# A two-layer MLP block in seven-product form on one core: the row norm ahead of it, the loads of its second phase and its last 512 hidden units rearranged

## The reference, cut to what matters

```python
x = x + y @ w_out[l]                                  # 1024 x 1024 by 1024 x 1024
xn2 = _rmsnorm(x, norm2_g[l])                          # row norm, the MLP's input
x = x + jnp.square(jax.nn.relu(xn2 @ w_up[l])) @ w_down[l]   # 1024 -> 4096 -> 1024
return _rmsnorm(x, final_g)
```

## Time and profile before

| what | value |
|---|---|
| median of 3 executions | 2787.88 us (2782.99 to 2789.32) |
| the profiled execution's own time | 2788.39 us |
| its span in the profile | 2786.6 us |
| mean granted clock of PE | 0.973 |
| output phase, second half, ends | at 2096.1 us |
| up phase, PE's last matmul | at 2429.3 us |
| down phase, first matmul | at 2437.55 us |
| PE's last matmul | at 2757.2 us |

### The profile page before, as it was taken

One profiled execution on the slowest core, in us unless ns is written; L12 is line 12 of the kernel. 1 busy time (PEld: TensorE's weight loads), 2 busy tenths in 40 slices (PEclk: granted clock), 3 DMA queues, 4 the chain that ended last, 5 costly groups with the idle time before them and its releaser, 6 DMA issues. The chain is left out here.

```text
span 2786.6 us, 37933 instructions
## 1 busy us (share of the span) xinstructions
PE 2614.4 (94%) x14936; PEld 2159.8 (78%) x14936; DVE 1758.1 (63%) x2677; ACT 1058.1 (38%) x1999; POOL 861.1 (31%) x582
## 2 busy tenths in 40 slices
PE   6999999999998999999989989999998999889995
PEld 4789888888866798888878768856686877668884
DVE  4312575676544413766765546868648787789998
ACT  3201233666522311335656334278613222233332
POOL 0000100234531001101326400046104656577665
PEclk8999999999999999999999999999999999999998
DMA  7322222136565222321264421100301434454441
GB/s 281 97 87 82 80 76 80 38 92 213 181 233 208 96 77 71 99 80 49 63 216 158 167 98 47 40 16 1 144 1 57 158 134 163 166 184 152 145 159 68
DMA packets 182255, 317.23 MB, mean 114 GB/s; under 512 B 29138, under 2 KB 110724, under 8 KB 174016
## 3 DMA queue, kind: packets, MB, share of 16 engines
q1 hardware_dynamic: 160928, 300.08, 31.9%
q10 hardware_dynamic: 21152, 14.75, 1.7%
HBM read 237.04 MB, written 72.50 MB: 111 GB/s over the span
## 5 line engine op out<-in xcount | busy, mean ns | idle before, releaser
L1026 PE MATMUL ps<-xn_hi_sb,ft_hi_sb 128*128 128x512 f32 (+1 forms) x720 | 264.0, 367 | 1.0 <-DVE ft_lo_sb L1477 1.0
L1027 PE MATMUL ps<-xn_lo_sb,ft_hi_sb 128*128 128x512 f32 (+1 forms) x720 | 263.2, 366 | 0.0
L1028 PE MATMUL ps<-xn_hi_sb,ft_lo_sb 128*128 128x512 f32 (+1 forms) x720 | 262.9, 365 | 0.0
L978 PE MATMUL ps<-tm_hi_sb,xn_hi_sb 128*128 128x512 f32 (+2 forms) x608 | 216.0, 355 | 14.8 <-DVE xn_lo_sb L1391 6.7
L980 PE MATMUL ps<-tm_hi_sb,xn_lo_sb 128*128 128x512 f32 (+2 forms) x608 | 213.3, 351 | 0.0
L979 PE MATMUL ps<-tm_lo_sb,xn_hi_sb 128*128 128x512 f32 (+2 forms) x608 | 213.1, 350 | 0.0
L2285 POOL TENSOR_TENSOR arena_sb<-arena_sb 128x1024 f32<-128x1024 f32 x10 | 25.9, 2591 | 418.7 <-ACT arena_sb L2000 418.7
L1026 PEld LDWEIGHTS ps<-xn_hi_sb,ft_hi_sb 128*128 128x128 f32 x720 | 136.8, 190 | 23.4 <-DVE ft_lo_sb L1477 1.4
L1027 PEld LDWEIGHTS ps<-xn_lo_sb,ft_hi_sb 128*128 128x128 f32 x720 | 136.9, 190 | 21.6
L1028 PEld LDWEIGHTS ps<-xn_hi_sb,ft_lo_sb 128*128 128x128 f32 x720 | 136.8, 190 | 21.7
L2081 ACT ACTIVATE arena_sb<-ps,neg_max_sb 128x640 f32<-128x640 f32 (+1 forms) x144 | 109.3, 759 | 103.7 <-DVE neg_max_sb L1644 97.7
(11 more groups left out here) (491 smaller groups left out, 7505.4 us busy)
## 6 DMA issues: line engine op xcount, KB each, us to landing
arena_sb<-in_w_ft SPq DMA_DIRECT2D x44, 512.0 KB, 3.3
arena_sb<-mqk_dram SPq DMA_DIRECT2D x36, 512.0 KB, 3.7
arena_sb<-x_dram SPq DMA_DIRECT2D x33, 512.0 KB, 7.0
arena_sb<-in_w_ada SPq DMA_DIRECT2D x16, 1024.0 KB, 9.0
u_raw_sb<-in_w_up SPq DMA_DIRECT2D x16, 1024.0 KB, 4.9
hq_dram<-h_part_sb SPq DMA_DIRECT2D x16, 1024.0 KB, 4.1
d_raw_sb<-in_w_down SPq DMA_DIRECT2D x16, 1024.0 KB, 5.6
xn_raw_sb<-hq_dram SPq DMA_DIRECT2D x32, 512.0 KB, 3.6
```

Of the source, the lines that this page charges most:

```text
L978: pe.matmul(at, hi, tm_hi[b][:, k, :], start=k == 0, stop=False)
L1026: pe.matmul(to, hi, xn_hi_flat[:, k, at:at + size], start=k == 0, stop=False)
L1027: pe.matmul(to, hi, xn_lo_flat[:, k, at:at + size], start=False, stop=False)
L1028: mm = pe.matmul(to, lo, xn_hi_flat[:, k, at:at + size], start=False, stop=k == KT - 1)
```

## The change

**Row norm.** The seven DVE operations of a tile become five, in three pieces put between the steps of the next tile's norm; ACT copies the upper half of a turned tile to SBUF (for tiles 0 to 3 one copy more). T4's second operation goes from POOL to DVE. The lo and hi parts of up's seventh weight block are made earlier, and PE turns tile 6 before and tile 7 after the first product of group 0.

**Up.** POOL starts the sums of a group's hidden blocks after three of the four are there; DVE begins the next group after three of the four sums; h12 is stored with the sums.

**Down.** `DN_ORDER` is 1, 2, 6, 5, 3, 7, 4, the preparation follows the products' order, and SP's order changes. The last pass is made by 16 plain units of 12 matmuls (192 in all) without block sums, with the joins of the sums beside them.

```diff
-                    sp.wait_ge(u_h, 4 * g + 4)
-                    sp.dma_start(hq_dram[g // 2][:, 0:3, g % 2, :], h_part[:, 0:3, :]).then_inc(hq_a, 16)
+                    sp.wait_ge(u_h, 4 * g + 2)
+                    sp.dma_start(hq_dram[g // 2][:, 0:2, g % 2, :], h_part[:, 0:2, :]).then_inc(hq_a, 16)
...
                 for w in range(1, WIDE):
                     load_hidden(w, 0)
+                    load_hidden(w, 1)
                     sp.wait_ge(t_sum, 4 * w - 1)
                     sp.wait_ge(q_lo, 9 * w - 7)
                     load_down(w, 0)
+                    load_hidden(w, 2)
+                    load_hidden(w, 3)
+                    if w < LAST:
+                        load_hidden(w, 4)
                     sp.wait_ge(t_sum, 4 * w)
-                    sp.wait_ge(q_lo, 9 * w - 1)
+                    sp.wait_ge(q_lo, 9 * w - 2)
                     load_down(w, 1)
-                    for j in range(1, 7):
-                        load_hidden(w, j)
+                    if w < LAST:
+                        load_hidden(w, 5)
+                        load_hidden(w, 6)
...
-            LOW_DVE = ((0, 0), (0, 1), (2, 0), (2, 1), (3, 1), (1, 1), (4, 1), (5, 1), (6, 1))
-            LOW_POOL = (3, 1, 4, 5, 6)
+            LAST = WIDE - 1
+            LOW_DVE = ((0, 0), (0, 1), (1, 0), (1, 1), (2, 1), (3, 1), (4, 1), (5, 1), (6, 1))
+            LOW_POOL = (2, 3, 4, 5, 6)
...
+                    def last_product(t, c):
+                        i, row, rows = 28 * LAST + 2 * t + c, t // 4, slice(t % 4 * P, (t % 4 + 1) * P)
+                        if t % 4 == 0:
+                            pe.wait_ge(q_lo, 9 * LAST + 6)
+                            pe.wait_ge(q_lop, 5 * LAST + 2)
+                        to = ps[:, (i + 4) % 8, :]
+                        pe.wait_ge(q_add, i - 7)
+                        for m in range(2):
...
                     if g > 0:
                         dve.wait_ge(hq_a, 16 * g)
-                        dve.wait_ge(u_hs, 4 * g)
+                        dve.wait_ge(u_hs, min(4 * g - 1, 4 * (GROUPS - 2)))
...
+                    adds(0)
                     low_quad(w, *LOW_DVE[7])
+                    adds(1)
                     low_quad(w, *LOW_DVE[8])
+                    adds(2)
+                    lows(0, 1)
...
+                    adds(3)
+                    lows(2, 3)
+                    adds(4)
+                    lows(4)
+                    adds(5)
+                    lows(5, 6)
+                    adds(6)
...
+                def last_down():
...
+                    dve.wait_ge(q_add, 28 * LAST)
+                    for t in range(4):
+                        join(sum6[t], sum1[t])
...
+                    for t in range(NX):
+                        add(t, 0)
+                        if t > 0:
+                            finish(t - 1)
+                        add(t, 1)
+                    finish(NX - 1)
...
+                        if 1 <= t <= 4:
+                            low_rows("2", xn2_hi, xn2_lo, t - 1)
+                        elif t > 4:
+                            first_rows(t - 1)
+                        mean_square("2", t)
+                        if t > 4:
+                            second_rows(t - 1)
+                        scale_row("2", x_res[:, t, :], g2_row, nx_s2[t % 2], t)
+                        if t > 4:
+                            third_rows(t - 1)
...
+                def last_joins(t):
+                    for c, what in ((0, sum6), (0, sum7), (1, sum5), (1, sum7)):
...
+                for t in range(4):
+                    last_joins(t)
+                    root("f", t)
```

More of the change, by code:

```diff
@@ L455, in build @@
         h_part = apart("h_part", W2 + 4096, 8, HALF)
-        h11, h12, h22, hs1, hs2, hs3, hs4, h21 = [h_part[:, i, :] for i in range(8)]
-        p1_copy, u_two, u_four = small[:, 0:HALF], small[:, HALF:2 * HALF], small[:, 2304:2304 + HALF]
+        h11, h22, hs1, hs3, hs2, h12, hs4, h21 = [h_part[:, i, :] for i in range(8)]
+        u_two, p1_copy = [apart(name, M2 + 17984 + HALF * i, HALF) for i, name in enumerate(("u_two", "p1_copy"))]
+        u_four = small[:, 2304:2304 + HALF]
         WIDE = D_FF // (2 * FG)
@@ L2630, in _ @@
                 load_down(0, 1)
-                for j in range(1, 7):
+                for j in range(1, 5):
                     load_hidden(0, j)
                 store_hidden(GROUPS - 1)
+                for j in range(5, 7):
+                    load_hidden(0, j)
                 store_sums(GROUPS - 1)
@@ L2996, in product @@
                             mm.then_inc(q_mm2, 1)
-                    for w in range(WIDE):
+                    def last_product(t, c):
[6 more added lines that the diff above has]
+                        for m in range(2):
+                            a, b = 2 * row + m, 2 * c + m
+                            for k in range(2):
+                                pe.matmul(to, aq_hi[a][:, k, rows], bq_hi[b][:, k, :], start=m == 0 and k == 0, stop=False)
+                                pe.matmul(to, aq_hi[a][:, k, rows], bq_lo[b][:, k, :], start=False, stop=False)
+                                mm = pe.matmul(to, aq_lo[a][:, k, rows], bq_hi[b][:, k, :], start=False, stop=m == 1 and k == 1)
+                        mm.then_inc(q_mm2, 1)
+                    for w in range(LAST):
                         for j in range(7):
                             product(w, j)
+                    for t in range(NX):
+                        for c in range(2):
+                            last_product(t, c)
                 projections()
@@ L3380, in up @@
                     else:
-                        for m in range(4, 7):
+                        for m in range(2, 7):
                             low_quad(0, *LOW_DVE[m])
@@ L3409, in add, with adds, lows @@
                             dve.tensor_tensor(x, x, ps[:, (i + 4) % 8, :], ALU.add).then_inc(q_add, 1)
-                    def join(to, what):
+                    def adds(j):
                         for t in range(4):
-                            dve.tensor_tensor(to(t), to(t), what[t], ALU.add).then_inc(q_both, 1)
+                            add(j, t)
+                    def lows(*which):
+                        for m in which:
+                            if w + 1 < LAST or m < 6:
+                                low_quad(w + 1, *LOW_DVE[m])
@@ L3429, in down @@
-                    for t in range(4):
-                        add(2, t)
+                    adds(2)
+                    lows(0, 1)
                     if w == 0:
                         dve.wait_ge(hq_a, 16 * GROUPS)
[L3433 to L3438, removed]
-                        join(lambda t: sum5[t], sum6)
-                    else:
-                        low_quad(w + 1, *LOW_DVE[2])
-                        low_quad(w + 1, *LOW_DVE[3])
@@ L3443, in down @@
-                    if w == 0:
-                        dve.wait_ge(hq_s, 16 * GROUPS)
-                    for t in range(4):
-                        add(4, t)
-                    if last:
-                        dve.wait_ge(q_both, 8)
-                        join(lambda t: x_res[:, t, 512:1024], sum5)
-                        dve.wait_ge(q_add, 28 * w + 20)
-                        dve.wait_ge(q_join, 8)
-                        join(lambda t: x_res[:, 4 + t, 0:512], sum7)
-                    else:
-                        low_quad(w + 1, *LOW_DVE[4])
@@ L3455, in down @@
-                    if last:
-                        dve.wait_ge(q_both, 12)
-                    for t in range(4):
-                        add(5, t)
-                    if last:
-                        dve.wait_ge(q_join, 12)
-                        join(lambda t: x_res[:, 4 + t, 512:1024], sum7)
-                        return
-                    low_quad(w + 1, *LOW_DVE[5])
-                    for t in range(4):
-                        add(6, t)
-                    low_quad(w + 1, *LOW_DVE[6])
@@ L3493, in _ @@
                     up(g)
-                for w in range(WIDE):
+                for w in range(LAST):
                     down(w)
-                finish()
+                last_down()
             @block.scalar
@@ L3801, in down @@
                 def down(w):
-                    for j in PREP:
+                    for j in range(4 if w == LAST else 7):
                         high_quad(w, j, 0)
```

230 lines of the change are left out of this document (123 added, 107 removed).

## The result

The changed kernel takes 2872.4 us (median of 4 runs, 2863.8 to 2873.7), the kernel before 2786.5 beside it (4 runs, 2783.0 to 2789.3): a ratio of 1.030, 95% interval 1.028 to 1.033. It is slower, as forecast, but by 3% instead of 1%: 2814 was forecast, and the range ended at 2832.

A forecast was written before the change was run, and what follows sets the result against it. The prediction took PE's matmuls plus PE's waits to bound the kernel. From 2788.4 us, -9 (row norm) - 8 (up) - 7 (passage) + 54 (down) - 4.5 (last pass and tail) gave 2814 us, range 2778 to 2832.

The forecast's parts named there:

- Up: Up phase, 15 groups: with POOL and DVE starting earlier the loop falls under PE's pace, gain 8 us, bounds 6 and 9.
- Row norm: End of the row norm: fewer DVE operations and T4's second operation on DVE gain 9 us, bounds 6 and 10.
- Passage: From up to down: hidden block no longer the wait, DVE's lo parts late instead; gain 7 us, bounds 4 and 16.
- Down: Passes 0 to 6: late half 1 of the weights adds waits, 9.05 us a pass, 54 us, bounds 37 and 71.
- Last pass and tail: Last pass to span end: 192 matmuls instead of 168, joins beside them; gain 4.5 us, bounds 0 and 9.
- rival of the other side: Down: SP's late transfer is covered, so only the gains are left, 2760 us; chance 0.17.
- (a): Passage and down: the added wait is there but bare, POOL and DVE miss each other, 2788 us; chance 0.15.
- (b): The rival of the other side: in down SP's late transfer is covered, 2760 us; chance 0.17.
- (d): The whole kernel: the forecast's own case, with all its terms, 2798 to 2832 us; chance 0.60.

The follow-up runs named there:

- e1: The changed kernel with POOL's sums of a group's hidden blocks again waiting for all four blocks, DVE's looser wait kept: 2815.8 us.
- e6: The changed kernel with late sums and early half 1 of down's weights, plus DVE draining down's first product ahead of two lo parts: 2766.0 us.
- e3: The changed kernel with SP loading half 1 of the next pass's down weights right behind half 0, ahead of hidden blocks 2 to 4: 2813.6 us.
- e5: The changed kernel with POOL's T2 in down waiting until DVE has made the lo part of block 3: 760.7 us from the turn of tile 7, 7.5 less.
- e2: The changed kernel with SP issuing the store of the sums only after the next weights' load has landed, sums still early: 2843.8 us.

## Why the prediction was wrong

**The step that failed is "Up".** It said: DVE starts each group 3.9 us late for POOL's fourth sum, "a loop of DVE's work and POOL's sums sets the pace", and with both looser the loop falls under PE's. The term was -8, its bounds -6 and -9; it measured +50.4. The loop I described exists, and freed of it up does gain 8.2 (e1). But I moved two waits and costed one. For POOL's earlier start I asked only what it releases, not what it stands beside: DVE's fourth to sixth lo parts, which POOL had not held up before, and SP's load, which the store of the sums now follows at once. Both lie in a second loop, load to last lo part to next load. It was as long as the first in the kernel before (19.6 us from 2401.55 to the end of the last lo part), and its load stood in the chain of waits of that kernel. The port's price for exactly such a pair I had used myself in the paragraphs behind it, for the passage and for down. The rule of the Trainium skill's page "SBUF — State Buffer", section "Who interferes with whom", that I cited there (issue order decides who is blocked) speaks against early sums just as well. The trace agrees: POOL's sum starts at 2314.09, ahead of the second of the two lo parts, and the two take 2.37 instead of 1.28. And the bounds of the term were drawn as if nothing could be lost there, so the range had no place for it.

**The rest of the sum held.** Without up's error it reads -8.2 - 8.2 - 6.4 + 55.4 - 4.8 = +27.8 against +25.5. Here 55.4 is six passes of 47.3 instead of 38.07, -4.8 is the last stretch's -6.3 with the 1.5 us by which the last pass starts late, and -6.4 is what is left of the third stretch for the passage. e1, which is the change without the early sums, took 2815.8 us against the forecast's 2814.

Row norm: -9 forecast, -8.2 measured. Behind output's last unit 9.8 us are gained (9.9 forecast), and the second half of output takes 1.6 longer (1 forecast). The wait of 3.3 at the turn stayed, products 2, 3 and 5 followed without a wait, and the last product waited 1.5.

Passage: 7 forecast, 6.4 measured. Its waits are 4.9, 1.7 and 4.9; I had 10.2, 2.9 and none, so the waits were wrong one by one, and their sum (11.5 against 13.1) came out near by luck. The hidden block is indeed no longer what PE waits for. The third wait I had ruled out; it is DVE's queue of lo parts at 3.3 to 3.4 us, and e6 shows that another order only moves it.

Down: the place, the cause and the size were right. First waits of 5.1 (5.7 forecast), second ones of 2.2 falling to 1.0 (1.65), a pass of 47.3 (47.15). Slow matmuls cost more than my 1.7 a pass, 2.5, the waits 6.7 instead of 7.35. e3 takes out the cause alone and gives back 8.2 of the 9.2 us a pass, e5 takes out POOL's operation ahead of the lo part.

Last pass and tail: -4.5 forecast, -4.8 measured; tiles 4 to 7 follow one another at 3.9 as assumed. The row norm and this part were read from the two traces only; no run undid either.

The rival of the other side (SP's late transfer is covered) fell with e3. That two semaphore counts of one edit can have opposite signs was in none of the rivals. Among the chances one sum was off: a third of (a) and (b) make 0.22 for faster, not 0.20, and slower should have been 0.71 where (d)'s low end is counted as no change.

## What to carry to other kernels

An earlier start is an edit in its own right: for each instruction that a loosened wait lets go sooner, list what it will then lie beside (its port, the DMA that it releases and what that follows), not only who waits for it. A wait of an engine that is listed as long, like DVE's 3.9 us a group here, says little about the pace if the engine would otherwise wait for something else; look in the chain of waits for every loop that closes within the period, and compare their lengths. And compare single traces from a common event just ahead of the change, since here PE's arrival there differed by 10 us between traces whose code ahead of it was the same. It must be one that the change itself does not move: the turn of tile 7, which the change puts one product earlier, would have made the row norm's gain 7.2 instead of 8.2 us.

## What was not expected of the hardware

A load of 1024 KB landed after 4.7 to 4.9 us (the median of each trace) with a store of 1280 KB (1024 KB before) issued 3.8 us or more behind it, and after 6.3 to 6.4 with that store 0.4 us behind it on the same queue; e2, which moves only the store, gives the difference back. So a transfer issued later on SP's queue lengthened the one ahead of it.

After every wait of 3.0 us and more in the ten traces from 2096 us on, PE ran some matmuls at 1.2 GHz (records of 0.63 us, as in the earlier trace rows). They need not be the first ones: behind the wait of 4.00 in e5 above, the first record has 0.47 us and seven of the next eight 0.63. After waits near 2.1 us it went either way. In e2 one of 2.14 was followed by seven of 0.63 us, another of 2.14 (before 2354.97) by none:

```profile
2376.75 0.50 PE L2972 MATMUL ps<-xn_hi_sb,uq_hi_sb 128*128 128x512 f32 x1 [2.14 <-DVE uq_lo_sb L3305]
...
2377.88 0.63 PE L2973 MATMUL ps<-xn_lo_sb,uq_hi_sb 128*128 128x512 f32 x1
```

In up of the changed kernel, waits of up to 4.0 us in 14 groups left 19.4 us of slow matmuls, 1.4 each.
